# Reordering the four products of a contraction step: long and short products in turn, one short product held over to the next step

## What is computed

```python
proj = jnp.einsum('bsd,de->bse', h, w_in[l])
u = jax.nn.relu(jnp.einsum('bsd,df->bsf', h, w_up[l]))
x = x + jnp.einsum('bsf,fd->bsd', u * u, w_down[l])
```

## Time and profile before

| | |
|---|---|
| median of 3 runs | 3415.55 us (3411.66 to 3417.08) |
| the profiled execution, its own time | 3416.99 us |
| its span, first to last instruction | 3415.2 us |
| TensorE matmuls, share of the span | 99% |
| TensorE weight loads | 84% |
| VectorE, ScalarE, GpSimd | 66%, 47%, 20% |
| data moved | 627.90 MB, mean 184 GB/s |

### The profile page before, as it was taken

How to read it: one execution, slowest core, us unless ns; L and a number is a source line. 1 busy time by engine, 2 the same in 40 slices (tenths; PEclk the granted TensorE clock), 3 DMA queues, 4 the chain that set the end, 5 groups by cost and what they waited for, 6 DMA issues and landing times. The chain is left out here.

```text
span 3415.2 us, 45081 instructions
## 1 busy us (share of the span) xinstructions
PE 3395.1 (99%) x18380; PEld 2859.8 (84%) x18380; DVE 2239.2 (66%) x2182; ACT 1600.0 (47%) x1787; POOL 693.2 (20%) x595
## 2 busy tenths in 40 slices
PE   9999999999999999999999999999999999999999
PEld 7888888888888888888888888888988888888887
DVE  6667646464655667646464658887767476885786
ACT  5555334333344555334333345744455444564564
POOL 1231000000000231000000000391000069672660
PEclk9999999999999999999999999999999999999999
DMA  6354555555555354555555555555544455455554
GB/s 234 141 192 165 194 187 186 193 187 187 195 185 182 145 191 161 189 192 186 188 193 185 192 196 182 185 196 186 184 165 160 169 186 202 174 197 185 183 200 154
DMA packets 95935, 627.90 MB, mean 184 GB/s; under 512 B 11564, under 2 KB 13868, under 8 KB 22672
## 3 DMA queue, kind: packets, MB, share of 16 engines
q1 hardware_dynamic: 84176, 601.92, 48.8%
q0 software_dynamic: 4096, 12.47, 1.4%
q10 hardware_dynamic: 7488, 11.01, 1.0%
HBM read 621.09 MB, written 2.17 MB: 182 GB/s over the span
## 5 line engine op out<-in xcount | busy, mean ns | idle before, releaser
L2639 PE MATMUL ps<-act,whi 128*128 128x512 f32 x4384 | 1365.9, 393 | 6.8 <-DVE wlo L1590 6.0
L1590 DVE TENSOR_TENSOR wlo<-raw,whi 128x2048 fp32r<-128x2048 f32 x400 | 929.5, 2347 | 456.3 <-ACT whi L1072 412.7
L2642 PEld LDWEIGHTS ps<-act,wlo 128*128 128x128 f32 x4384 | 823.1, 188 | 182.1
L1072 ACT ACTIVATE whi<-raw 128x2048 fp32r<-128x2048 f32 x342 | 653.3, 1914 | 520.1 <-DMA raw<-in_w_down 305.0
L2642 PE MATMUL ps<-act,wlo 128*128 128x256 f32 x4384 | 865.7, 279 | 0.0
L2639 PEld LDWEIGHTS ps<-act,whi 128*128 128x128 f32 x4384 | 665.5, 188 | 11.2 <-issue 9.8
L953 ACT ACTIVATE whi<-raw 128x2048 fp32r<-128x2048 f32 x226 | 430.5, 1913 | 270.2 <-DMA raw<-in_o_w_in 93.8
L1597 DVE TENSOR_TENSOR wlo<-raw,whi 128x2048 fp32r<-128x2048 f32 x168 | 395.4, 2358 | 126.7 <-ACT whi L953 126.4
L2597 PE MATMUL ps<-whi,act 128*128 128x512 f32 x1152 | 456.3, 396 | 0.1
L2599 PE MATMUL ps<-whi,act 128*128 128x512 f32 x1152 | 455.4, 395 | 0.0
L2598 PE MATMUL ps<-wlo,act 128*128 128x512 f32 x1152 | 455.4, 395 | 0.0
(11 more groups left out here) (477 smaller groups left out, 4476.8 us busy)
## 6 DMA issues: line engine op xcount, KB each, us to landing
raw<-in_w_up SPq DMA_DIRECT2D x128, 1024.0 KB, 4.8
raw<-in_w_down SPq DMA_DIRECT2D x128, 1024.0 KB, 4.8
raw<-in_o_w_in SPq DMA_DIRECT2D x80, 1024.0 KB, 4.8
raw<-in_e_w_in SPq DMA_DIRECT2D x64, 1024.0 KB, 4.8
raw<-in_w_in SPq DMA_DIRECT2D x59, 1024.0 KB, 4.8
raw<-in_w_o SPq DMA_DIRECT2D x32, 1024.0 KB, 4.8
raw<-in_e_w_out SPq DMA_DIRECT2D x32, 1024.0 KB, 4.8
raw<-in_o_w_out SPq DMA_DIRECT2D x32, 1024.0 KB, 4.8
```

What stands on the lines that cost most here:

```text
L1072: act.activation(whi[:, slot, :], raw[:, slot, :], ACT.Copy).then_inc(sem("hi_ready"), 1)
L1590: dve.tensor_tensor(wlo[:, slot, :], raw[:, slot, :], whi[:, slot, :].bitcast(F32), ALU.subtract).then_inc(sem("lo_ready"), 1)
L2639: pe.matmul(ps[:, b + f, :], whi[:, slot, cols[f]], a[:, kt, :, :].rearrange("p a t -> p (a t)"), start=(kt == 0), stop=False)
L2642: ins = pe.matmul(ps[:, b + f, S:2 * S], wlo[:, slot, cols[f]], a[:, kt, 0, :], start=False, stop=(kt == KT - 1))
```

## The change

In both functions the loops of a step are rewritten. After long 0 of a step comes short 1 of the step before (held over), then long 1, then short 0. The first step of a slot has no short 1 before it; the last step of a slot issues short 0 and short 1 at its end. The banks in turn are b, b + 1, b + 1, b. The products themselves, their operands, their number and the semaphores stay as they are.

```diff
@@ products
-                        cols = [slice(i * GC + f * P, i * GC + f * P + P) for f in range(2)]
                         for f in range(2):
-                            pe.matmul(ps[:, b + f, :], whi[:, slot, cols[f]],
+                            at = i * GC + f * P
+                            pe.matmul(ps[:, b + f, :], whi[:, slot, at:at + P],
                                       a[:, kt, :, :].rearrange("p a t -> p (a t)"), start=(kt == 0), stop=False)
-                        for f in range(2):
-                            ins = pe.matmul(ps[:, b + f, S:2 * S], wlo[:, slot, cols[f]], a[:, kt, 0, :],
+                            if f == 0 and i:
+                                pe.matmul(ps[:, b + 1, S:2 * S], wlo[:, slot, at - P:at], a[:, kt - 1, 0, :],
+                                          start=False, stop=False)
+                        for f in range(2 if i == TK - 1 else 1):
+                            at = i * GC + f * P
+                            ins = pe.matmul(ps[:, b + f, S:2 * S], wlo[:, slot, at:at + P], a[:, kt, 0, :],
                                             start=False, stop=(kt == KT - 1))
@@ feature_part
-                            cols = [slice(a * GC + f * P, a * GC + f * P + P) for f in range(2)]
                             for f in range(2):
-                                pe.matmul(ps[:, b + f, :], whi[:, slot, cols[f]],
+                                at = a * GC + f * P
+                                pe.matmul(ps[:, b + f, :], whi[:, slot, at:at + P],
                                           act0[:, kt, :, :].rearrange("p a t -> p (a t)"), start=(kt == 0), stop=False)
-                            for f in range(2):
-                                ins = pe.matmul(ps[:, b + f, S:2 * S], wlo[:, slot, cols[f]], act0[:, kt, 0, :],
+                                if f == 0 and a:
+                                    pe.matmul(ps[:, b + 1, S:2 * S], wlo[:, slot, at - P:at], act0[:, kt - 1, 0, :],
+                                              start=False, stop=False)
+                            for f in range(2 if a == TK - 1 else 1):
+                                at = a * GC + f * P
+                                ins = pe.matmul(ps[:, b + f, S:2 * S], wlo[:, slot, at:at + P], act0[:, kt, 0, :],
                                                 start=False, stop=(kt == KT - 1))
```

## The result

| | before | changed |
|---|---|---|
| median | 3415.78 us (4 runs, 3411.66 to 3417.08) | 3437.03 us (4 runs, 3435.55 to 3438.39) |
| ratio | | 1.0065, 95% interval 1.0053 to 1.0077 |
| span of the profiled execution | 3415.2 us | 3436.6 us |

The change costs 21.3 us. The forecast was a gain of 14.6, and the range ended at 3425; the time is that of rival C (3439).

The account below looks back on a forecast made before the run. TensorE's back-to-back product stream was taken as the bound. Alternation was to give -14.6 us and all other terms were taken as 0, so the median of 3415.55 us would become 3401 us, range 3389 to 3425.

Parts of the forecast that it names:

- rival C: Steps of four products fall into the slow 0.70 us rhythm: +10 ns a step, +23.8 us, 3439 us; chance 0.20 for all sizes.
- What bounds the kernel: TensorE's matmuls fill 99% of the span; 2384 steps at 0.690 us make 1645 us, 48%; supply isn't the bound.
- the banks: In the new order each short product is followed by a long one into the same bank; costed at nothing.
- The waits for low parts: Line 2639's waits for low parts of the weights, 6.0 us, were to grow by 0 to +2 us, taken as 0.
- the one named: Stretch from 2800 to 3300 us, called the busiest for VectorE of those cut, at 365 of 500 us.
- a gain beyond the additive one: A gain in the product steps larger than the summed neighbour savings; some 0.05 chance, left out of the range.
- point 3: In the steps, neighbours of the other kind make products cheaper: -7.0 ns on each of 2086 steps, -14.6 us.
- The 0.70 at the edge of a stage: After another kind of product, three steps run at 0.70 us before the 0.69 rhythm; read as more than one rhythm.
- Rival B: In the steps, the new order costs and gives nothing: 690 ns a step as before, 3415.5 us; chance 0.33.
- Rival D: The gain goes into waits for weights at the heads of slots, leaving 3415.5 us; chance 0.03.

Follow-up runs that it names:

- e3_starts: Kernel of bare product streams, against the first such kernel with two plain fp32 products ahead of each stream, other beginnings and moved tiles; pairs at the kernel's place 690.0 ns a step.
- e1_streams: Kernel of 21 bare product streams, no layer computed, only TensorE at work, against the full kernel; pairs 696.7 ns a step, held-over orders 706.7.

## Why the prediction was wrong

*What bounds the kernel* stands: the stream's distances of starts are the time, 1 ns on a step 2.4 us. The waits, the clock and the other engines had no part in the loss, and the banks, set at nothing, cost nothing in either kind of kernel. The waits for low parts, set at 0 to +2 us, fell by 5.4. Two slips changed nothing: the stretch from 2200 to 2440 us was busier for VectorE (187 of 240 us) than the one named, and the 0.05 for a gain beyond the additive one has no place in the four rivals' chances, which fill 1 without it.

*The failed step is point 3, "What alternation is worth".* I took the difference between a mixed step (228.5 and 116.5) and streams of one kind (233 in the earlier trace rows, 117.7 in the earlier trace rows) for a saving that a neighbour of the other kind brings, and doubled it. It measured +11.7 ns a step by the starts (+9 with what the rest gave back, 21.3 us / 2384), where -7.0 was forecast for seven eighths of the steps. It failed in two ways. First, the two rows weren't comparable: the 233 of the wide stages belongs to their place, and is 226.7 at another, while the mixed step's 690 belongs to the pairs at distance 64. I noted that the long row came from the other kind of stream and answered that by taking a middle between two prices of the short product, which left the doubt about the long one untouched. A difference between streams that differ in more than the neighbour is no price of the neighbour.

The rows that were missing lie in the trace of `e3_starts`: streams of long and of short products alone, weights held, both tiles at the kernel's place.

```profile
L427 PE MATMUL ps<-act,whi x80: 388/392/478, 633.5 to 651.6; 128*128 128x512 f32 x80
...
L438 PE MATMUL ps<-act,wlo x80: 279/279/365, 652.2 to 661.6; 128*128 128x256 f32 x80
```

Behind their first starts they run at 228.9 and 117.8 ns, so a mixed long product (228.5) is 0.4 ns cheaper than in its own kind, not 4.5, and a short one (116.5) 1.3. Second, the doubling fails even with these prices: 2 x 228.9 + 2 x 117.8 is 693.4 ns, the pairs take 3.4 less, and the orders in turn, which should take 3.4 less again, take 698 or 707.

*Rival C* had the right sign and, at its full size, the time: 3439 against 3437.03. That it comes so near is partly luck: it set 10 ns on every step where 11.7 were lost, and no gain in the waits where 6.5 us came back. The 0.70 at the edge of a stage was the sign in the trace that the same products have more than one rhythm. I gave its full size too little chance because it was rare. Its guess at a cause, the short product followed by a long one into the same bank, is refuted. *Rival B* (each product has its fixed price) is refuted as well. The formula of the Trainium skill that I set beside it ("TensorE: Matmul & The Clock Gate", section "Back-to-back issue gap") doesn't describe these streams either: by estimate it gives 216 ns for 512 columns, where the runs show 226.7 to 233.3 for wide products by place alone. I left out that the same section calls it the gap of an isolated matmul and gives about 131 ns for 512 columns in a stream of loads and matmuls; no run here shows that figure. *Rival D* didn't occur: nothing was gained, and the waits fell.

What the runs show: at the kernel's place the pairs have one rhythm, 690 ns a step, and any order in turn that was tried falls, wherever nothing stands between its steps, into one of two, 698 or 707. Over the eight steps between seams that is 5.59 or 5.66 us against 5.52. What lies behind it is only argued. The quantum of 6.67 ns is, at 2.4 GHz and 4 bytes a column, the time in which a product streams 64 bytes; over 256 bytes the effect begins anew, with four values at the multiples of 64 bytes (none between them was tried); and a load runs beside each product, beginning with it. This fits a load and a stream that read the same part of memory in turns of 64 bytes and hold each other up. No run separates the two reads, for instance by streams that keep their weights, so it stays open, as does what picks the rhythm at a beginning.

## What to carry to other kernels

Before reordering a matmul stream that is already back to back, look at the distances of single starts, not at means of groups: if they repeat in a pattern with a fixed quantum, the stream has rhythms, and an edit of the order may pick a worse one. A price taken from another stream holds only at the same places of its tiles, and what one neighbour saves, two needn't save twice; try a tile 64, 128 and 192 bytes further before any reordering, for it costs no instruction and here it was worth 0.84%, more than the reordering lost. Kernels of bare streams, one run each, settled what rows of the full kernel couldn't.

## What was not expected of the hardware

The distance between the weight tile and the activation tile modulo 256 bytes moves a product of 512 columns between 226.7 and 233.3 ns, and a step of four products, in one and the same order, between 690.0 and 696.7. Identical code on identical tiles runs at 698 ns a step in one stage and at 707 in another. The best place depends on the stream: distance 0 for wide products, 64 for the pairs with held weights. Counted from the held tile to the streamed one, long products agree whichever operand is held, in the two cases where both were run: 226.7 ns at 0 (`longs` in `e1_streams`, and the wide products at 0), and 228.9 at 64 (the long products alone above, and the wide products in the column of 192).
